# Two-layer hybrid block and pooled/attention block on one core: half of the second layer's modulation moved into that layer, and six Winograd pairs put into the first feed-forward stage

## The reference, cut to what matters

```python
c_act = silu(c)
mod = c_act @ w_ada + b_ada                      # 1024 -> 6144, one row
shift1, scale1, gate1, shift2, scale2, gate2 = split(mod, 6)
h = rms_norm(x, norm1_g) * (1 + scale1) + shift1
...                                              # retention, forgetting attention, GLA from h @ w_in
y_br = einsum('bsnw,nwd->bsnd', branches, w_br)
gates = sigmoid(h @ w_mg + b_mg)                 # 1024 -> 3 x 1024
x = x + gate1 * (sum_n(gates * y_br) @ w_o)
h2 = rms_norm(x, norm2_g) * (1 + scale2) + shift2
u, g = split(h2 @ w_up, 2)                       # 1024 -> 2 x 2816
x = x + gate2 * ((silu(causal_dwconv(u)) * g) @ w_down)
```

## Time and profile before

| | us |
|---|---|
| median of 3 runs | 2883.38 |
| lowest, highest | 2878.95, 2883.96 |
| the profiled execution, its own time | 2879.27 |
| its span in the trace | 2877.5 |
| TensorE busy | 2828.5 (98%) |
| VectorE busy | 1760.0 (61%) |
| ScalarE busy | 1218.6 (42%) |
| GpSimd busy | 1100.4 (38%) |

### The profile page before, as it was taken

One profiled execution on the slowest core, in us unless ns is written; L12 is line 12 of the kernel. 1 busy time (PEld: TensorE's weight loads), 2 busy tenths in 40 slices (PEclk: granted clock), 3 DMA queues, 4 the chain that ended last, 5 costly groups with the idle time before them and its releaser, 6 DMA issues.

```text
span 2877.5 us, 38581 instructions
## 1 busy us (share of the span) xinstructions
PE 2828.5 (98%) x16103; PEld 2412.5 (84%) x16103; DVE 1760.0 (61%) x2394; ACT 1218.6 (42%) x1861; POOL 1100.4 (38%) x447
## 2 busy tenths in 40 slices
PE   8999989999999999999999999999999999999999
PEld 5777879888888877789998988888989877789998
DVE  6444588667674624447766755648668466676683
ACT  4336334442333434544444434444334466443433
POOL 2332333434445433243435344543334423333432
PEclk9999999999999999999999999999999999999999
DMA  8331344346664332233333333333333322233332
GB/s 259 104 103 51 103 139 140 109 141 200 195 201 142 103 83 66 67 95 100 92 101 93 98 106 88 103 96 92 101 109 103 102 67 67 74 94 97 108 103 76
DMA packets 507297, 314.32 MB, mean 109 GB/s; under 512 B 14290, under 2 KB 478836, under 8 KB 506868
## 3 DMA queue, kind: packets, MB, share of 16 engines
q1 hardware_dynamic: 507124, 311.87, 36.9%
HBM read 309.73 MB, written 2.10 MB: 108 GB/s over the span
## 4 chain that ended last, share of the span: by engine, by line
PE 90%; DVE 5%; ACT 1%; DMA 1%; issue 1%; SPq 1%; POOL 0%; DVEq 0%; ACTq 0%
PE b L514 14%; PE b L516 14%; PE b L515 14%; PE s L514 3%; PE s L515 3%; PE s L516 3%; PE b L1251 3%; PE b L1253 3%; PE b L1252 3%; PE o L514 3%; PE o L515 3%; PE o L516 3%; PE s L1251 2%; PE s L1253 2%; PE s L1252 2%; PE b L1189 1%
## 5 line engine op out<-in xcount | busy, mean ns | idle before, releaser
L3483 POOL TENSOR_TENSOR lo<-raw,hi 128x1024 fp32r<-128x1024 f32 (+3 forms) x437 | 1098.1, 2523 | 1747.9 <-ACT hi L1528 1275.4
L1528 ACT ACTIVATE hi<-raw 128x1024 fp32r<-128x1024 f32 (+1 forms) x440 | 449.9, 1034 | 304.0 <-DMA raw<-in_w_up_dram 94.4
L514 PE MATMUL b<-HH,hi 128*128 128x512 f32 x1088 | 436.5, 401 | 1.6 <-DVE X L2413 1.6
L516 PE MATMUL b<-HH,lo 128*128 128x512 f32 x1088 | 424.3, 390 | 0.0
L515 PE MATMUL b<-HL,hi 128*128 128x512 f32 x1088 | 424.2, 390 | 0.0
L514 PEld LDWEIGHTS b<-HH,hi 128*128 128x128 f32 x1088 | 204.2, 188 | 52.1 <-issue 7.1
L516 PEld LDWEIGHTS b<-HH,lo 128*128 128x128 f32 x1088 | 204.2, 188 | 43.8
L515 PEld LDWEIGHTS b<-HL,hi 128*128 128x128 f32 x1088 | 204.5, 188 | 42.1 <-issue 1.4
L514 PE MATMUL b<-FH,hi 128*128 128x512 f32 (+1 forms) x391 | 144.8, 370 | 1.5 <-POOL lo L3483 1.5
L515 PE MATMUL b<-FL,hi 128*128 128x512 f32 (+1 forms) x391 | 144.5, 370 | 0.0
L516 PE MATMUL b<-FH,lo 128*128 128x512 f32 (+1 forms) x391 | 144.5, 369 | 0.0
(11 more groups left out here) (768 smaller groups left out, 7492.6 us busy)
## 6 DMA issues: line engine op xcount, KB each, us to landing
raw<-in_w_up_dram SPq DMA_DIRECT2D x88, 512.0 KB, 4.1
raw<-in_w_ada_dram SPq DMA_DIRECT2D x80, 512.0 KB, 4.9
raw<-in_w_in_dram SPq DMA_DIRECT2D x76, 512.0 KB, 4.0
raw<-in_w_mg_dram SPq DMA_DIRECT2D x48, 512.0 KB, 3.9
raw<-in_ffn_w_gate_dram SPq DMA_DIRECT2D x44, 512.0 KB, 3.8
raw<-in_ffn_w_up_dram SPq DMA_DIRECT2D x44, 512.0 KB, 3.8
raw<-in_w_down_dram SPq DMA_DIRECT2D x32, 448.0 KB, 3.7
raw<-in_ffn_w_down_dram SPq DMA_DIRECT2D x32, 448.0 KB, 4.0
```

The lines of the kernel that those rows point to most:

```text
L514: e.matmul(out, wh, xh, start=start and k == 0, stop=False)
L516: mm = e.matmul(out, wl, xh, start=False, stop=stop and k == last)
L1528: e.activation(t["hi"][:, c % NSLOT, 0:w], K.raw[:, c % NSLOT, 0:w], ACT.Copy).then_inc(*m.hi.up(c))
L3483: e.tensor_tensor(t["lo"][:, s, 0:w], K.raw[:, s, 0:w], t["hi"][:, s, 0:w].bitcast(F32), ALU.subtract).then_inc(*m.lo.up(n))
```

## The change

Modulation: 6 steps more in the input tiles of the retention part of each layer, 22 instead of 28 in the mixing; the second layer gets a modulation generator of its own for groups 6 to 11 (48 steps), so that the first feed-forward has 62 steps instead of 110. The second layer's fold takes four groups instead of three. Stage 0 gets six pairs, and BUSY in units 6, 7 and 14. The preparation of the activations' block sums is taken apart: one instruction each at more places, in the mixings (units 2 to 4) and in stages 0 and 1. In the mixings, unit 3's gate tiles and all of unit 4 now say BUSY.

```diff
-PAIRS_OF = ((),
+PAIRS_OF = ((8, 9, 10, 15, 16, 17),
             (7, 8, 9, 11, 12, 14, 15, 16, 18, 19),
...
+SUMS_AT = (3, 4)
+WHOLE_TILES = (6, 7, 14, KF - 1)
...
-ADA_LAST = ((6, 9, 11), (3, 7, 11))
+ADA_LAST = ((6, 9, 11), (3, 6, 9, 11))
...
-        drain(P.ret_inputs(l))
+        ada = (y for q in range((4, 6)[l], 12) for y in P.ada(l, q))
+        drain(beside(P.ret_inputs(l), ada, 6))
         drain(P.ret_values(l))
-        ada = (y for q in range(4, 12) for y in P.ada(0, q)) if l == 0 else iter(())
...
-        drain(beside(P.mixing(l, range(2, 12)), ada, 28))
+        drain(beside(P.mixing(l, range(2, 12)), ada, 22))
...
-                for q in range(12):
+                for q in range(6):
                     yield from P.ada(l + 1, q)
...
 # TensorE, mixing
-                        yield BUSY if f == 4 else None
+                        yield BUSY if f in SUMS_AT else None
...
-                yield from self.dot(self.bank[b][:, :], terms, [key] + ([("chunk", c)] if u else []),
-                                    (m.lo.at(c), self.free[b]))
+                for _ in self.dot(self.bank[b][:, :], terms, [key] + ([("chunk", c)] if u else []),
+                                  (m.lo.at(c), self.free[b])):
+                    yield BUSY if f == 4 else None
...
 # all engines, feed-forward
-                        yield BUSY if f == KF - 1 else None
+                        yield BUSY if f in (WHOLE_TILES if i == 0 else (KF - 1,)) else None
...
 # ScalarE, mixing
             if f == 3:
-                self.halves_high(i, (0, 1, 2))
+                self.halves_high(i, (0,))
...
+                    if f == 3:
+                        self.halves_high(i, (1 + u,))
...
 # ScalarE, feed-forward
-            if j == 3 and PAIRS_OF[i]:
+            if i == 0 and j in (13, 14):
+                self.halves_high(i, (2 * j - 26, 2 * j - 25))
+            if i > 1 and j == 3:
                 self.halves_high(i)
+            if i == 1 and 5 <= j <= 8:
+                self.halves_high(i, (j - 5,))
...
 # VectorE, mixing
             if f == 2:
-                self.halves_whole(i)
-            if f == 3:
-                self.halves_sums(i)
+                self.halves_whole(i, (0,))
...
+                if f == 2:
+                    self.halves_whole(i, (1,))
+                if f == 3:
+                    self.halves_sum(i, 1)
+                if f == 4:
+                    self.halves_low(i, (1,))
...
+                if f == 2:
+                    self.halves_whole(i, (2,))
                 if f == 3:
-                    self.halves_low(i, (0, 1, 2))
+                    self.halves_sum(i, 2)
                 if f == 4:
-                    self.halves_low(i, (3,))
+                    self.halves_low(i, (2,))
...
             branch(0)
+            if f == 2:
+                self.halves_whole(i, (3,))
+            if f == 3:
+                self.halves_sum(i, 3)
...
             branch(1)
+            if f == 2:
+                self.halves_sum(i, 0)
+            if f == 3:
+                self.halves_low(i, (0,))
+            if f == 4:
+                self.halves_low(i, (3,))
...
+    def halves_step(self, i, j):
+
+        spread = i == 1
+        if i == 0 and j in (10, 11):
+            self.halves_whole(i, (j - 10,))
+        elif i == 0 and j == 12:
+            self.halves_whole(i, (2, 3))
+        elif i == 0 and j in (13, 14):
+            self.halves_sum(i, 2 * j - 26)
+            self.halves_sum(i, 2 * j - 25)
+        elif i == 0 and j == 15:
+            self.halves_low(i, range(4))
+        elif i == 0:
+            return
+        elif spread and 1 <= j <= 4:
+            self.halves_whole(i, (j - 1,))
+        elif spread and 5 <= j <= 8:
+            self.halves_sum(i, j - 5)
+        elif spread and 9 <= j <= 12:
+            self.halves_low(i, (j - 9,))
...
```

More of the change, by code:

```diff
@@ L1982, in mixing @@
                     for _ in self.tile():
-                        yield BUSY if f == 4 else None
+                        yield BUSY if f in SUMS_AT else None
                     sigmoid(u)
+                    if f == 3:
+                        self.halves_high(i, (1 + u,))
             self.chunk()
-            yield None
-            yield None
+            yield BUSY if f == 4 else None
+            yield BUSY if f == 4 else None
             for d in (2 * dp, 2 * dp + 1) if n == 1 else ():
@@ L2130, in ffn @@
                     for _ in self.tile():
-                        yield BUSY if f == KF - 1 else None
-                    self.ffn_jobs(i, j)
+                        yield BUSY if f in (WHOLE_TILES if i == 0 else (KF - 1,)) else None
+                    take(j)
             else:
@@ L3022, in ffn_jobs, with halves_whole @@
             self.ffn_conv(i, j // 2)
-    def halves_whole(self, i):
+    def halves_whole(self, i, js=range(4)):
         e, q, m, t = self.e, self.q, self.m, self.t
-        for j, (k, c) in enumerate(((0, 0), (0, 256), (4, 256), (4, 0))):
+        for j in js:
+            k, c = ((0, 0), (0, 256), (4, 256), (4, 0))[j]
             q.wait_ge(m.vnorm.at("h", ffn_norm(i), 1, 7))
@@ L3030, in halves_whole, with halves_sum @@
                             t["HL"][:, k:k + 4, c:c + 256].bitcast(F32), ALU.add).then_inc(*m.vtake.up(("whole", i, j)))
-    def halves_sums(self, i):
+    def halves_sum(self, i, j):
         e, q, m = self.e, self.q, self.m
[L3035 to L3043, removed]
+        R1, R3, R2, R4 = [self.K.sums_of(i, n)[2] for n in range(4)]
+        if j == 0:
+            q.wait_ge(m.vtake.at("whole", i, 1))
+            e.tensor_tensor(R1, R3, R1, ALU.subtract).then_inc(*m.vtake.up(("traw", i, 0)))
+        elif j == 1:
+            q.wait_ge(m.vtake.at("whole", i, 2), m.vtake.at("traw", i, 0))
+            e.tensor_tensor(R3, R2, R3, ALU.subtract).then_inc(*m.vtake.up(("traw", i, 1)))
+        elif j == 2:
+            q.wait_ge(m.vtake.at("traw", i, 1))
+            e.tensor_tensor(R2, R1, R2, ALU.subtract).then_inc(*m.vtake.up(("traw", i, 2)))
+        else:
+            q.wait_ge(m.vtake.at("whole", i, 3), m.vtake.at("traw", i, 2))
+            e.tensor_tensor(R4, R4, R2, ALU.add).then_inc(*m.vtake.up(("traw", i, 3)))
@@ new lines, in halves_step @@
+    def halves_step(self, i, j):
[17 more added lines that the diff above has]
+            self.halves_low(i, (j - 9,))
+        elif not spread and j == 2:
+            self.halves_whole(i)
+        elif not spread and j == 3:
+            for n in range(4):
+                self.halves_sum(i, n)
+        elif not spread and j in (4, 5):
+            self.halves_low(i, (2 * j - 8, 2 * j - 7))
@@ L3129, in take @@
             if PAIRS_OF[i]:
[L3130 to L3135, removed]
+                self.halves_step(i, j)
         gate = self.t["MOD"][:, i, 40:48] if i < 2 else None
```

6 lines of the change are left out of this document (3 added, 3 removed).

## The result

The changed kernel takes 2891.41 us (median of 6 runs, 2890.19 to 2894.31) against 2879.77 for the kernel before in the same session: ratio 1.0036, 95% interval 1.0024 to 1.0048. It is slower, by 11.6 us. Forecast were 2881.7 and no measurable change. The profiled execution took 2890.47 us, its span 2888.7, 11.2 more than before.

A forecast was written before the change was run, and what follows sets the result against it. TensorE, busy 98% of the span, was taken as the bound. Costs of 15.8 us less gains of 17.5 gave -1.7: 2877.6 us profiled, 2881.7 for the median; own range 2876 to 2889, with rivals 2868 to 2892.

The forecast's parts named there:

- Mixing, first layer: First layer's mixing: the first fold's stop and slow clock go, 7.3 us, and the pair's two stops, 3.7 us.
- Six pairs: Stage 0: six pairs save 0.83 us of TensorE work each, 5.0 us.
- The pairs behind the down parts: Stage 0, units 8 and 15: pairs stop because VectorE prepares their weight sums late, costing 6.5 and 5.1 us.
- Moved block sums in stages 0 and 1: Stages 0 and 1: same instructions, lag covered by free buffers of three units; cost nothing, 0 to 1 us.
- Retention inputs: Retention inputs of both layers: six modulation steps delay the value product behind them, 1.0 us per layer, 2.0 us.
- second layer: Second layer's 48 steps: cost 1.1 us in forget-attention values, 0.8 at the output projection, 0.3 for the extra fold.
- the wait at 920: End of stage 0: a wait for a weight behind the last modulation chunks goes, gaining 1.5 us.
- The clock: Behind the two groups of pairs: halved clock, 1.8 us each, counted only in the slower rival.
- faster, the pairs don't stop: Rival: stage 0's pairs behind the down parts run without stops, 11.6 us come off, 2870; chance 0.31.
- Waiting fold: Rival: a fold still waits in the mixing, 7.3 us or more return, about 2889 to 2893; chance 0.08.
- Slower: Rival: GpSimd fully blocks VectorE at stage 0's pairs and the clock falls, 2892.7 us; chance 0.20.
- the stretch of 1.4: VectorE's instructions beside GpSimd in the first layer's down part: taken as lengthened 1.4 times on average, not fully blocked.

The follow-up runs named there:

- e7: Changed kernel without its six pairs and without the second layer's 48 moved steps, the mixing's block sums made in bulk as before: 2871.55 us, ratio 0.9967.
- e3: Changed kernel without modulation beside the last three tiles of each down part of stage 0: 2880.48 us, ratio 0.9998 to the kernel before.
- e4: Changed kernel with the edits of e2 and e3 together: 2872.61 us, ratio 0.9972 to the kernel before.
- e2: Changed kernel with stage 0's four low parts made one per down tile, behind the modulation, instead of together: 2887.62 us, ratio 1.0021 to the kernel before.
- e6: e4 without modulation in the second layer's retention inputs: 2875.33 us, ratio 0.9978 to the kernel before.
- e1: Changed kernel without its six pairs in stage 0 and the block sums and BUSY that go with them: 2875.15 us, ratio 0.9977 to the kernel before.

## Why the prediction was wrong

The sum was -1.7 us; the spans differ by +11.2. (The 4.1 us that were added for the median were the spread of three runs; over six runs the median is only 0.5 above the profiled execution.) By its own steps:

- *Mixing, first layer*, -7.3 and -3.7: measured -10.96. Right in size. But the reason given joined two causes; e7 shows that the earlier fold and the emptier unit 4 suffice.
- *Six pairs*, 6 x 0.83 = 5.0: 0.79 each, 4.8. Right.
- *The pairs behind the down parts*, 6.5 and 5.1: measured 6.4 and 5.5, but only with the clock, which the sum did not have. The idle time alone was 5.0 and 3.5, some 1.5 us less in each, so that the sizes agree is partly luck. The form was right: first a stop for GpSimd's lo at the start of each unit (3.20 and 3.02 us), then one for `MP` (1.80 and 0.43), and VectorE idle for a transfer, 5.01 us, ahead of unit 8's sums.
- **The step that failed: "*Moved block sums in stages 0 and 1*: same instructions ... free buffers of three units cover them ... Nothing, 0 to 1 us."** It cost 8.1 us by e3's pieces (6.8 came back when e4 took it away). I asked only whether TensorE's output buffers cover VectorE's lag, and there they do. I did not ask what else waits for VectorE: the slots of the ring that its modulation chunks hold. The four low parts stand directly ahead of them, and the in-order queue carries VectorE's lag over to down weights that have nothing to do with the sums. A little above, I had used that very queue, for the pair of unit 5. This term is 8.1 of the 12.9 us between forecast and result.
- *Retention inputs* and *second layer*, together 2.0 + 1.9 + 0.3, against 1.5 for the wait at 920, which did go. Right for the value products: 1.02 us in the first layer, 1.08 and 0.91 in the second. The 0.8 at the second layer's output projection did not come. Too low by some 4 us in all: +1.41 ahead of the first mixing where 1.0 stood; a wait of 1.04 us in the second layer's weave of retention and forget inputs, at 1034.58 for VectorE's `fq`, and one of 0.65 for `retR`, in both layers, were not listed; and in the second mixing the idle time before unit 11's `mEH` half product grew from 0.68 to 1.96. That the second layer "carries the first layer's load at the same places" missed that unit 11 has a pair there. The 0.70 us behind the first mixing and the 0.74 in the remainder, one each way, are within what a single span varies.
- *The clock*: it was priced only in the slower rival. Behind the stop of 5.6 us the granted clock is 0.50, 1.2 of 2.4 GHz, and 0.72 on average behind unit 15's of 3.02. The forecast had a stop of 3 us in each group and no clock for it. It was also down at unit 8's start: 0.50 behind 3.20 us.

The rivals: *faster, the pairs don't stop* would be e4, once both causes are removed by hand (2872.6 against 2870). *Waiting fold* did not happen, there is no wait for `AS` in either mixing. *Slower*, 2892.7, gave nearly the right time by the wrong way: it wanted 19.0 us and 3.6 of clock in the two groups, which took 11.9 with the clock. The ports between VectorE and GpSimd matter all the same. In the 8.47 us of the four low parts, which alone take 1.22 each, 4.9, GpSimd runs for 2.91 and 2.81 us, against 2.12 undisturbed: while both ran, 5.7 us, they did some 6.4 us of work. They all but took turns, and that is a better price than the stretch of 1.4 that I took, but it did not decide. The Trainium skill, "SBUF — State Buffer", section "SBUF: two separate sides", states that whichever of the two starts first holds the shared ports for the whole instruction and the other fully blocks. The trace nearly agrees: strict turns would be 5.7 us of work in the 5.7, not 6.4.

That it is the place of the four low parts, in one block ahead of the modulation, and not their number that makes the first stop is shown by e2 and e4, which make the same four. How long the DMA queue's own part of the delay is, from the issue at 674.09 to the split at 679.66, stays open: it was not varied, and no run had another transfer size or ring depth.

## What to carry to other kernels

A block of work that moves is hidden only if everything queued behind it is: the consumer's output buffers, and also the ring slots that the same engine must free, since an in-order DMA queue hands one slot's lateness to every transfer behind it, however unrelated. When work is spread into slots between other work, count the slots: a few steps left over are made in a row at the worst place, and four of them cost the piece in which they landed 7.5 us (e6), where the 48 of e1 cost 3.7 in the whole. And before building a change of many parts, run each alone: here one part, the first layer's placement, held the whole gain, and the others as first built took back twice as much.

## What was not expected of the hardware

The wait that the profile names stood far from its cause: TensorE waited for GpSimd, idle for 10.51 us itself, which waited for ScalarE, for a DMA that was not issued because VectorE was busy. Stops give time back: without the 5.6 us stop, the next one grew from 3.20 to 5.10 us, since TensorE came to it 6.3 us earlier and the sums only 4.4. And a short stop costs more than itself: behind 5.62 us idle the clock was at 1.2 GHz, and behind 3.02 us it was already down for part of the next 6 us (0.72). With it the stop of 5.29 us in e3 made its piece 8.1 us longer. Around 2 us it goes either way: one and the same stop in the second mixing, 1.96 us in the change and 1.98 in e4, left the clock over the next 3.4 us at 1.00 in the first and at 0.62 in the second. The mixing takes 206.95 us in the one and 208.39 in the other, all of the difference in busy time (204.99, 206.41).
